# Two chains of a chunked recurrence, one head parity after the other or both side by side, on one core

## The chip, the cores and the metric

The kernel runs on one core of a Trainium2 chip. The metric is device time in microseconds: the median of three runs, and one execution more is taken with the hardware profiler. The core has a matmul engine (TensorE, PE in the rows), two elementwise engines (VectorE, DVE; ScalarE, ACT), GpSimd (POOL) and the queue that starts transfers (SyncE, SP). Each works through its own list in order and waits on semaphores. Matmul results go to eight PSUM banks of 128 x 512 floats; the other tiles lie in SBUF.

## What is computed

Two transformer blocks over 256 tokens of width 1024. The change is in the second one's time mixing, a recurrence with 8 heads of 64 dimensions; all the rest (convolution, attention, expert layers, gates) is untouched.

```python
def rwkv7_scan(r, w, k, v, a, b):
    def step(state, inp):
        rt, wt, kt, vt, at, bt = inp
        sa = jnp.einsum("bhij,bhj->bhi", state, at)
        state = state * wt[:, :, None, :] + sa[..., None] * bt[:, :, None, :] + vt[..., None] * kt[:, :, None, :]
        return state, jnp.einsum("bhij,bhj->bhi", state, rt)
    state0 = jnp.zeros((B, H, N, N), jnp.float32)
    _, ys = lax.scan(step, state0, xs)
    return jnp.swapaxes(ys, 0, 1)
...
    y = rwkv7_scan(r_h, heads(decay), k_h, v_h, -kk, kk * a_h)
    m = jnp.mean(y, axis=-1, keepdims=True)
    var = jnp.mean(jnp.square(y - m), axis=-1, keepdims=True)
    yn = ((y - m) * lax.rsqrt(var + GN_EPS)).reshape(B, S, D_RWKV)
    ...
    out = (yn + bonus) * g
...
    mixed = (gate_a * (y_attn @ w_branch_attn) + gate_b * (y_rwkv @ w_branch_rwkv)) @ w_out
```

## The kernel before

All matrices live transposed: features on partitions, tokens along a row. The recurrence isn't stepped token by token. It is done in four chunks of 64 tokens, and two chunks (128 tokens, index `a` = 0 or 1) share one set of matrices. Tiles `at_`, `bt_`, `kt_`, `rt_` hold decayed a, b, k and r: four tiles of 128 partitions, two heads in each, the even head on partitions 0 to 63 and the odd one on 64 to 127 (`q` = 0 or 1).

For each `a` and then each `q` the kernel runs one chain over four heads at a time:

- outer products over 64 partitions (`outer`, L536): `A`, `At`, `Mak`, later `Arb` and `Ark`, each masked by VectorE (L768). `At` masked to 16 x 16 blocks (L775) is the matrix to be inverted, plus identity (L779) the first `X`;
- three levels: squares `S2` and `S2t` of the block matrix (L544), copied to SBUF by ScalarE (L670, L673), and `XS`, the square times X, added to X by VectorE (L786);
- `ZV` (L552), the k part of the chunk times the values, copied by L666;
- two joining rounds, 16 to 32 and 32 to 64: `TR` transposes X (L569, copy L677), `Q` is the off-diagonal mask of `At` (L791) times that (copy L679), `XQ` is Q times X, added at L786.

After both chains of an `a` come the two chunks' state steps: `P` = a times state (L583), plus ZV (L799); `ys` = state times r (L586); `U` = X times that (L590, copy L686); `S` = k,v and b,U products (L597, L598), then VectorE adds it to the state `Sbd`, masks it to the two heads' diagonal blocks (L805) and decays it (L807). `Sbd` is 128 x 512, half of it zeros. At the end `yu` (L607, L608) gives the part of the output from U and v, copied and added into `yT` (L689, L812). Group norm statistics (L612) of y follow, then the gate columns `gb`, the branch `wb` and `w_out`.

One set of tiles (`XA`, `mS`, `mSt`, `mAt`, `mT`, `ArbT`, `ArkT`, `ZV`) serves all chains. TensorE jobs take banks 0 to 3 in turn (`take`, group A), `ys` banks 6 and 7, `yu` 4 and 5; a taken bank waits for the instruction that last read it. The order on every engine is the order of the code.

Weights come through a ring of six 1 MB slots (`ring_raw`), loaded in order by SP as soon as the unit six before has been split by ScalarE and VectorE. When the recurrence begins, `gb` 0 and 1 have been split, and their two slots hold `w_out` 0 and 1.

## Time and profile before

| | us |
|---|---|
| runs, three | 2598.78, 2600.93, 2603.32 |
| median | 2600.93 |
| profiled execution, own time | 2601.82 |
| its span, first to last instruction | 2600.1 |
| mean granted TensorE clock | 0.931 |
| recurrence, first ktok transpose to first group-norm matmul | 169.05 |

The page lists each engine's busy time; a timeline row is a start, a duration, engine, line, operation, what is written and read, and in brackets the engine's idle time before it and what ended that. An fp32 matmul leaves two records, so a job of four matmuls reads x8. The granted clock is given as a share of full speed, 1.00 or 0.50 at any moment, and a mean over a stretch.

### The profile page before, as it was taken

The page shows a single profiled execution, that of the slowest core. Times are in us where ns is not written, and L with a number is a line of the kernel's source. Part 1 is how long each engine was busy: PE and PEld are TensorE (multiplying, and loading weights), DVE is VectorE, ACT ScalarE, POOL GpSimd, SP SyncE. Part 2 cuts the span into 40 slices and gives each one's busy share as a digit, 9 for nine tenths or more (in the row PEclk, how much of TensorE's full clock was granted, in tenths as well). Part 3 has the DMA queues.
Part 4 walks back from the last instruction along what each step waited for, and adds up shares of the span by engine and source line. Part 5 has one row for each costly group of instructions (what it writes and reads, how often), then busy time and mean ns, then how long its engine had stood idle before and what let it go on. Part 6 is the DMA issues. An engine that isn't in the chain of part 4 may idle for free.

```text
span 2600.1 us, 33806 instructions
## 1 busy us (share of the span) xinstructions
PE 2342.4 (90%) x13490; PEld 1998.6 (77%) x13490; DVE 1746.8 (67%) x1709; ACT 1378.2 (53%) x1273; POOL 92.4 (4%) x147
## 2 busy tenths in 40 slices
PE   4997999799799999999999999879857786999986
PEld 3866999787688888888888888769657675888876
DVE  2764344634788888888888888554552265799954
ACT  2224333444477777777777777434421133677743
POOL 8300000001000000000000000000000000000000
PEclk6998999899799999999999999989777787999988
DMA  8566765366289999999999999766100031699940
GB/s 265 191 198 200 243 205 181 112 209 213 77 307 389 371 366 376 364 378 369 372 372 369 373 368 373 212 111 197 65 1 1 1 114 49 233 368 372 370 165 17
DMA packets 339243, 618.62 MB, mean 238 GB/s; under 512 B 24608, under 2 KB 165153, under 8 KB 339086
## 3 DMA queue, kind: packets, MB, share of 16 engines
q1 hardware_dynamic: 339086, 616.43, 67.9%
q8 instruction: 110, 1.80, 0.3%
q14 instruction: 47, 0.39, 0.0%
HBM read 614.26 MB, written 1.05 MB: 237 GB/s over the span
## 4 chain that ended last, share of the span: by engine, by line
PE 87%; DVE 7%; ACT 2%; issue 2%; SPq 1%; DMA 1%; DVEq 0%; POOL 0%; ACTq 0%; POOLq 0%
PE bank L945 10%; PE bank L946 10%; PE bank L947 10%; PE bank L1826 6%; PE bank L1827 6%; PE bank L1828 6%; PE bank L977 5%; PE bank L979 5%; PE bank L975 5%; PE bank L544 2%; PE bank L1863 1%; PE bank L1936 1%; PE bank L1897 1%; PE bank L918 1%; PE bank L1892 1%
## 5 line engine op out<-in xcount | busy, mean ns | idle before, releaser
L1150 DVE TENSOR_TENSOR ring_lo<-ring_raw,ring_hi 128x2048 fp32r<-128x2048 f32 x432 | 988.3, 2292 | 139.9 <-ACT ring_hi L1060 139.3
L1060 ACT ACTIVATE ring_hi<-ring_raw 128x2048 fp32r<-128x2048 f32 x432 | 828.1, 1920 | 288.8 <-PE bank L947 181.1
L945 PE MATMUL bank<-ring_hi,xg_hi 128*128 128x512 f32 x1152 | 458.0, 398 | 2.1 <-DVE xg_lo L1250 2.1
L946 PE MATMUL bank<-ring_hi,xg_lo 128*128 128x512 f32 x1152 | 451.0, 391 | 0.0
L947 PE MATMUL bank<-ring_lo,xg_hi 128*128 128x512 f32 x1152 | 450.8, 391 | 0.0
L1826 PE MATMUL bank<-Hh,ring_hi 128*128 128x256 f32 x1048 | 307.8, 294 | 55.9 <-DVE ring_lo L439 22.7
L439 DVE TENSOR_TENSOR ring_lo<-ring_raw,ring_hi 128x2048 fp32r<-128x2048 f32 (+1 forms) x96 | 218.0, 2282 | 189.2 <-ACT ring_hi L421 165.9
L1827 PE MATMUL bank<-Hl,ring_hi 128*128 128x256 f32 x1048 | 304.6, 291 | 0.0
L1828 PE MATMUL bank<-Hh,ring_lo 128*128 128x256 f32 x1048 | 304.1, 290 | 0.0
L1826 PEld LDWEIGHTS bank<-Hh,ring_hi 128*128 128x128 f32 x1048 | 209.6, 200 | 59.3 <-issue 48.1
L945 PEld LDWEIGHTS bank<-ring_hi,xg_hi 128*128 128x128 f32 x1152 | 217.5, 189 | 47.9 <-ACT xg_hi L1103 2.9
L947 PEld LDWEIGHTS bank<-ring_lo,xg_hi 128*128 128x128 f32 x1152 | 217.1, 188 | 47.1
L946 PEld LDWEIGHTS bank<-ring_hi,xg_lo 128*128 128x128 f32 x1152 | 217.5, 189 | 43.4
L421 ACT ACTIVATE ring_hi<-ring_raw 128x2048 fp32r<-128x2048 f32 (+1 forms) x96 | 181.4, 1898 | 109.5 <-PE bank L1828 78.8
L975 PE MATMUL bank<-ring_hi,mh 128*128 128x512 f32 x576 | 228.4, 396 | 0.0
L977 PE MATMUL bank<-ring_hi,mh 128*128 128x512 f32 x576 | 228.2, 396 | 0.0
L979 PE MATMUL bank<-ring_lo,mh 128*128 128x512 f32 x576 | 228.1, 396 | 0.0
L1827 PEld LDWEIGHTS bank<-Hl,ring_hi 128*128 128x128 f32 x1048 | 209.9, 200 | 0.1
L1828 PEld LDWEIGHTS bank<-Hh,ring_lo 128*128 128x128 f32 x1048 | 209.5, 200 | 0.0
L979 PEld LDWEIGHTS bank<-ring_lo,mh 128*128 128x128 f32 x576 | 108.4, 188 | 26.2
L977 PEld LDWEIGHTS bank<-ring_hi,mh 128*128 128x128 f32 x576 | 108.5, 188 | 25.8
L975 PEld LDWEIGHTS bank<-ring_hi,mh 128*128 128x128 f32 x576 | 108.4, 188 | 25.7
(439 smaller groups left out, 2916.6 us busy)
## 6 DMA issues: line engine op xcount, KB each, us to landing
ring_raw<-in_moe_w SPq DMA_DIRECT2D x672, 512.0 KB, 5.2
ring_raw<-in_ada_w SPq DMA_DIRECT2D x96, 512.0 KB, 5.9
ring_raw<-in_ffn_w SPq DMA_DIRECT2D x66, 512.0 KB, 5.3
ring_raw<-in_exp_gate SPq DMA_DIRECT2D x64, 512.0 KB, 5.2
ring_raw<-in_exp_up SPq DMA_DIRECT2D x64, 512.0 KB, 5.3
ring_raw<-in_exp_down SPq DMA_DIRECT2D x64, 512.0 KB, 5.6
ring_raw<-in_w_in SPq DMA_DIRECT2D x42, 512.0 KB, 4.9
ring_raw<-in_conv_in_w SPq DMA_DIRECT2D x16, 512.0 KB, 8.2
```

What stands on the lines that cost most here:

```text
L439: nc.vector.tensor_tensor(ring_lo[:, i % SPLIT, 0:kt * c], ring_raw[:, n % RAW, 0:kt * c], ring_hi[:, i % SPLIT, 0:kt * c].bitcast(F32), A ...
L945: mm(o, xg_hi[:, g, kk, :], wh(k), start=(kk == 0), stop=False)
L946: mm(o, xg_lo[:, g, kk, :], wh(k), start=False, stop=False)
L947: last = mm(o, xg_hi[:, g, kk, :], wl(k), start=False, stop=(kk == KT - 1))
L975: mm(o, mh_hi[:, 2 * h + k, :], wh[:, k, ns], start=begin, stop=False, skip_group_check=True)
L977: mm(o, mh_lo[:, 2 * h + k, :], wh[:, k, ns], start=False, stop=False, skip_group_check=True)
L979: last = mm(o, mh_hi[:, 2 * h + k, :], wl[:, k, ns], start=False, stop=end, skip_group_check=True)
L1060: run(ring_hi[:, s, :], ring_raw[:, n % RAW, :], ACT.Copy).then_inc(T.sem("hi_done"), 1)
L1150: tt(ring_lo[:, s, :], ring_raw[:, n % RAW, :], ring_hi[:, s, :].bitcast(F32), ALU.subtract).then_inc(T.sem("lo_done"), 1)
L1826: mm(o, wh[:, k, cs], Xh[:, k, :], start=(k == 0), stop=False)
L1827: mm(o, wh[:, k, cs], Xl[:, k, :], start=False, stop=False)
L1828: last = mm(o, wl[:, k, cs], Xh[:, k, :], start=False, stop=(k == kt - 1))
```

## The change

Each tile of a chain now exists twice, for q = 0 and 1: `mS`, `mAt`, `mSt` get a second copy in the bias table `relb` (rows name it relb), `mT` in `turn2`. For `a` = 1 there are `XA2`, `ZV2`, `ArbT2`, `ArkT2`, laid into the two ring slots that hold w_out 0 and 1; SP therefore loads w_out 0 only after the last `yu`. Jobs of even heads take banks 0 to 2 (`q0`), odd heads 3 to 5 (`q1`), outputs bank 6, U and S bank 7. The steps of the two chains are written side by side on all engines; the two state chunks of `a` = 0 are placed between the steps of `a` = 1; outer products are issued alternately for even and odd heads. The state `Sc` is compact, 128 x 256 without the zero blocks, so the masking pass is gone, and P, S and ys become 64 x 64 matmuls per head. y is gathered in one bank in three parts, `y_v`, `y_s`, `y_u`, and copied once by ScalarE.

```diff
+        GROUPS = {"A": [0, 1, 2, 3], "B": [4, 5], "C": [6, 7], "D": [4, 5, 6, 7],
+                  "q0": [0, 1, 2], "q1": [3, 4, 5], "state": [7], "y": [6]}
...
+            def outer(a, name, l, rr):
+                cs = slice(a * P, (a + 1) * P)
+                b = [take(pe, f"{name} {a} {q}", f"q{q}") for q in range(2)]
+                for i in range(4):
+                    for q in range(2):
+                        r = slice(64 * q, 64 * q + 64)
+                        last = mm(b[q][:, i * P:(i + 1) * P], l[r, i, cs], rr[r, i, cs], start=True, stop=True)
+                        if i == 3:
+                            last.then_inc(pe.tick(f"mm {name} {a} {q}"), 1)
...
+            def state_p(c):
...
+                for h in range(HEADS2):
+                    r, i, _ = of_head(h)
+                    last = mm(b[h % 2][b0, 64 * i:64 * i + 64], at_[r, i, t64], Sc[r, i, :], start=True, stop=True)
...
+                def body(b, h):
+                    r, i, hs = of_head(h)
+                    o = b[r, 64 * i:64 * i + 64]
+                    mm(o, ktok[b0, hs], Vtok[b0, a, hs], start=True, stop=False, skip_group_check=True)
+                    return mm(o, btok[b0, hs], U[b0, hs], start=False, stop=True, skip_group_check=True)
...
+            def y_s(c):
...
+                for h in range(HEADS2):
+                    r, i, _ = of_head(h)
+                    o = ps_y[a][r, i * P + 64 * (c % 2):i * P + 64 * (c % 2) + 64]
+                    mm(o, Sc[r, i, :], rt_[r, i, t64], start=False, stop=False,
+                       skip_group_check=True).then_inc(pe.tick(f"mm ys {c}"), 1)
...
+            tok(0)
+            strict(0)
+            squares(0, 0)
+            zv(0, 0)
+            squares(0, 1)
+            zv(0, 1)
+            reads(0)
+            for lev in range(3):
+                level(0, 0, lev)
+                level(0, 1, lev)
+            for o in range(2):
+                for step in (turn_x, joined, joined_x):
+                    step(0, 0, o)
+                    step(0, 1, o)
+
+            strict(1)
+            state_u(0)
+            squares(1, 0)
+            zv(1, 0)
+            state_s(0)
+            squares(1, 1)
+            zv(1, 1)
+            reads(1)
+            state_p(1)
+            level(1, 0, 0)
+            state_u(1)
+            level(1, 1, 0)
+            level(1, 0, 1)
+            state_s(1)
+            level(1, 1, 1)
+            level(1, 0, 2)
+            level(1, 1, 2)
+            y_v(0)
+            y_s(1)
...
+            joined_x(1, 1, 1)
+            state_u(2)
+            state_s(2)
+            state_p(3)
+            y_s(3)
+            state_u(3)
+            y_u(1)
...
+            def state_s(c):
+                dve.eng.wait_ge(*T.at(f"mm S {c}"))
+                if c:
+                    dve.eng.wait_ge(*T.at(f"mm ys {c}"))
+                tt(Sc, Sc, four(ps(f"S {c}")[:, 0:256]), ALU.add).then_inc(dve.tick(f"ev S {c}"), 1)
+                dve.eng.wait_ge(*dve.own())
+                tt(Sc, Sc, eLC[:, :, c].unsqueeze(2).to_broadcast([P, 4, 64]),
+                            ALU.mult).then_inc(dve.tick(f"S {c + 1}"), 1)
...
+                if key == ("w_out", 0):
+                    sp.eng.wait_ge(*T.at("mm yu 1"))
```

TensorE's list, at the end of the first half's second chain and the start of the state steps, before (bank numbers are PSUM banks; tB holds X, scr the state and U, GhF also Pm and the k and b columns; stat is mT, pr and prT are mS and mSt):

```order
L569 MATMUL bank0<-ident,tB 128x128 x4
L544 MATMUL bank1<-stat_54,prT 128x128 x4
L544 MATMUL bank2<-tB,pr 128x128 x4
L583 MATMUL bank3<-scr,tD 64x128 x4
L586 MATMUL bank7<-tA,scr 128x64 x4
L590 MATMUL bank0<-GhF_49,tB 64x64 x8
```

The same round after, with the first outer products of the second half behind them:

```order
L597 MATMUL bank0<-ident,tB 128x128 x4
L597 MATMUL bank3<-ident,tB 128x128 x4
L542 MATMUL bank1<-stat_54,prT 128x128 x4
L542 MATMUL bank4<-turn2_55,relb_57 128x128 x4
L542 MATMUL bank2<-tB,pr 128x128 x4
L542 MATMUL bank5<-tB,relb_57 128x128 x4
L556 MATMUL bank0<-tD,tC 128x128
L556 MATMUL bank3<-tD,tC 128x128
```

Every job has the other parity's job behind it, and the state steps have left this place; the outer products alternate between bank 0 and bank 3. Their new place on TensorE, within the second half's levels, after (L635 is U, L647 and L648 are S, L542 are S2, S2t and XS):

```order
L542 MATMUL bank0<-prT 128x128 x4
L542 MATMUL bank1<-prT 128x128 x4
L542 MATMUL bank2<-XA2_58,prT 128x128 x4
L635 MATMUL bank7<-GhF_49,tB 64x64 x8
L542 MATMUL bank3<-relb_57 128x128 x4
L542 MATMUL bank4<-relb_57 128x128 x4
L542 MATMUL bank5<-XA2_58,relb_57 128x128 x4
L542 MATMUL bank0<-pr,prT 128x128 x4
L542 MATMUL bank1<-XA2_58,pr 128x128 x4
L647 MATMUL bank7<-tB,GhF_49 64x64
L648 MATMUL bank7<-scr,GhF_49 64x64
```

U of chunk 1 now stands between the even and the odd heads' first level, and S two jobs later. VectorE's list at the start of a chain, before (L768 masks A, At, Mak, Arb, Ark; L786 adds to X):

```order
L768 TENSOR_TENSOR pr<-bank3,alibi 128x512
L768 TENSOR_TENSOR pr<-bank0,alibi 128x512
L768 TENSOR_TENSOR prT<-bank1,alibi 128x512
L775 TENSOR_TENSOR prT<-pr,alibi 128x512
L779 TENSOR_TENSOR tB<-prT,ident 128x4x128
```

and after, at the start of the second half:

```order
L929 TENSOR_TENSOR pr<-bank0,alibi 128x512
L936 TENSOR_TENSOR prT<-pr,alibi 128x512
L929 TENSOR_TENSOR relb_57<-bank3,alibi 128x512
L936 TENSOR_TENSOR relb_57<-relb_57,alibi 128x512
L929 TENSOR_TENSOR pr<-bank1,alibi 128x512
L940 TENSOR_TENSOR XA2_58<-prT,ident 128x4x128
L929 TENSOR_TENSOR relb_57<-bank4,alibi 128x512
L940 TENSOR_TENSOR XA2_58<-relb_57,ident 128x4x128
L929 TENSOR_TENSOR prT<-bank2,alibi 128x512
L929 TENSOR_TENSOR relb_57<-bank5,alibi 128x512
L971 TENSOR_TENSOR scr<-scr,bank7 128x256
L973 TENSOR_TENSOR scr<-scr,eLC 128x256
```

Six passes stand up to the first X where five stood, and the state's add and decay (L971, L973) follow before the masks of Arb.

## Rows read from the trace of the kernel before

**Rows 1.** The page, busy time, share of the span and instructions of each engine.

```profile
PE 2342.4 (90%) x13490; PEld 1998.6 (77%) x13490; DVE 1746.8 (67%) x1709; ACT 1378.2 (53%) x1273; POOL 92.4 (4%) x147
```

**Rows 2.** Table by stage of the recurrence: stretch, length, busy by engine, clock, DMA.

```profile
core 0: us, PE busy (x) PEld busy (x) DVE busy (x) ACT busy (x) POOL busy (x), PEclk, DMA share, GB/s
1906.50:1967.75 61.25, 44.46 (x312) 39.85 (x313) 20.41 (x31) 11.95 (x22) 0.00 (x0) 0.92 0.00 1
1967.75:1989.73 21.98, 18.38 (x129) 16.62 (x129) 5.53 (x8) 1.78 (x3) 0.00 (x0) 0.64 0.00 1
1989.73:2056.27 66.54, 49.77 (x315) 45.08 (x313) 19.47 (x29) 11.95 (x22) 0.00 (x0) 0.84 0.00 1
2056.27:2075.55 19.28, 14.74 (x113) 13.17 (x113) 4.14 (x6) 1.78 (x3) 0.00 (x0) 0.66 0.00 0
1906.50:2075.55 169.05, 127.36 (x865) 114.73 (x865) 49.54 (x74) 27.46 (x50) 0.00 (x0) 0.82 0.00 1
```

**Rows 3.** TensorE timeline, first half: transposes, products, a joining round, state steps.

```profile
1906.50 0.66 PE L529 MATMUL bank<-ident,tA 128*128 128x128 f32 x4 [0.87 <-DVE tD L748]
1906.99 0.60 PE L529 MATMUL bank<-ident,tC 128*128 128x128 f32 x4
...
1912.57 2.08 PE L544 MATMUL bank<-pr,prT 128*128 128x128 f32 x8 [2.10 <-DVE tB L779]
...
1949.45 2.05 PE L544 MATMUL bank<-prT 128*128 128x128 f32 x16
1951.34 1.06 PE L544 MATMUL bank<-tB,prT 128*128 128x128 f32 x8
...
1962.61 0.66 PE L569 MATMUL bank<-ident,tB 128*128 128x128 f32 x4 [0.78 <-DVE tB L786]
...
1967.75 1.09 PE L583 MATMUL bank<-scr,tD 128*64 128x128 f32 x8 [0.78 <-DVE tB L786]
...
1969.80 1.14 PE L590 MATMUL bank<-GhF,tB 64*64 64x64 f32 x16
1971.62 0.48 PE L597 MATMUL bank<-tB,GhF 64*128 64x128 f32 x2 [0.68 <-ACT scr L686]
...
1973.29 0.38 PE L598 MATMUL bank<-scr,GhF 64*128 64x128 f32 x2
1975.91 1.97 PE L583 MATMUL bank<-scr,tD 128*64 128x128 f32 x8 [2.23 <-DVE scr L807]
```

**Rows 4.** Groups by line: busy us, mean ns of one, idle before.

```profile
L679 ACT ACTIVATE pr<-bank 128x512 f32<-128x512 f32 x8 | 4.8, 597 | 10.1 <-PE bank L544 10.1
...
L2594 DVE SCALAR_TENSOR_TENSOR tA<-xT,bank 128x256 f32<-128x256 f32 x8 | 3.0, 419 | 17.1 <-PE bank L1828 17.1
```

**Rows 5.** VectorE timeline at the start of the first chain.

```profile
1910.50 0.69 DVE L768 TENSOR_TENSOR prT<-bank,alibi 128x512 f32<-128x512 f32 x1 [0.20 <-PE bank L536]
1911.11 0.68 DVE L775 TENSOR_TENSOR prT<-pr,alibi 128x512 f32<-128x512 f32 x1
1911.82 0.69 DVE L779 TENSOR_TENSOR tB<-prT,ident 128x512 f32<-128x512 f32 x1
```

**Rows 6.** TensorE's weight loads (PEld) and matmuls before the recurrence.

```profile
1868.60 0.18 PEld L508 LDWEIGHTS bank<-tB,scr 64*128 64x128 f32 x1
1868.61 0.18 PEld L510 LDWEIGHTS bank<-tB,scr 64*128 64x128 f32 x1
...
1868.61 0.48 PE L510 MATMUL bank<-tB,scr 64*128 64x256 f32 x1
...
1869.67 0.70 PE L514 MATMUL bank<-tB,scr 128*128 128x256 f32 x2
...
1871.07 0.59 PE L515 MATMUL bank<-tB,scr 128*128 128x256 f32 x2
```

**Rows 7.** Table by stage, the stretch of the second half's L607 and L608.

```profile
2070.87:2074.60 3.73, 3.73 (x32) 3.33 (x32) 0.00 (x0) 0.57 (x1) 0.00 (x0) 0.50 0.00 0
```

**Rows 8.** After the recurrence: ScalarE's split of w_out 0; SP's next transfers.

```profile
2116.77 1.90 ACT L421 ACTIVATE ring_hi<-ring_raw 128x2048 fp32r<-128x2048 f32 x1
...
2102.57 5.28 SPq L1702 DMA_DIRECT2D ring_raw<-in_w_out  x4
```

More of the change, by code:

```diff
@@ L490, in rwkv_pe, with job @@
             pe.stage = "rwkv"
-            def job(name, body, waits=()):
-                b = take(pe, name)
+            def job(name, body, waits=(), group="A"):
+                b = take(pe, name, group)
                 for label in waits:
@@ new lines, in reads, with level @@
+            def reads(a):
+                outer(a, "Arb", bt_, rt_)
+                outer(a, "Ark", kt_, rt_)
+            def level(a, q, lev):
+                n = f"{a} {q}"
+                pe.eng.wait_ge(*T.at(f"S2 {n} {lev}"))
+                power = mS[q][(lev + 1) % 2]
+                if lev < 2:
+                    job(f"S2 {n} {lev + 1}", prod(f4(mSt[q]), f4(power)), group=f"q{q}")
+                if lev < 1:
+                    job(f"S2t {n} {lev + 1}", prod(f4(power), f4(mSt[q])), group=f"q{q}")
+                pe.eng.wait_ge(*T.at(f"TX {n} {lev}"))
+                job(f"XS {n} {lev}", prod(f4(power), lambda i: XA[a][:, 2 * i + q, :]), group=f"q{q}")
@@ new lines, in state_u @@
+            def state_u(c):
+                b0, _ = by_chunk(c)
+                a = c // 2
+                if c % 2 == 0:
+                    for q in range(2):
+                        pe.eng.wait_ge(*T.at(f"TX {a} {q} 5"))
+                        pe.eng.wait_ge(*T.at(f"ev ZV {a} {q}"))
+                if c:
+                    pe.eng.wait_ge(*T.at(f"P {c}"))
+                src = Pm if c else ZV[0]
+                job(f"U {c}", each(8, lambda b, h: mm(b[b0, 64 * h:64 * h + 64], XA[a][b0, h, b0],
+                                                      src[b0, 64 * h:64 * h + 64], start=True, stop=True)), group="state")
@@ L651, in rwkv_act, with tok @@
             act.eng.wait_ge(*T.at("decayed"))
[L652 removed]
+            def tok(a):
                 for name, dst in (("ktok", ktok), ("btok", btok)):
@@ new lines, in y_out @@
+            def y_out(a):
+                act.eng.wait_ge(*T.at(f"mm yu {a}"))
+                run(yT[:, :, a * P:(a + 1) * P], four(ps(f"ys {a}")[:, :]), ACT.Copy).then_inc(act.tick(f"ev ys {a}"), 1)
+                T.mark(f"y {a}", *act.last)
+            tok(0)
+            for a in range(TT):
+                if a:
+                    state_u(0)
+                for q in range(2):
+                    zv(a, q)
+                    square(a, q, 0)
+                square(a, 0, 1)
+                if a:
+                    state_u(1)
+                square(a, 1, 1)
+                square(a, 0, 2)
+                square(a, 1, 2)
+                for o in range(2):
+                    turn_x(a, 0, o)
+                    turn_x(a, 1, o)
+                    joined(a, 0, o)
+                    joined(a, 1, o)
+                    if a and o == 0:
+                        tok(1)
+                        y_out(0)
@@ new lines, in reads, with add, off @@
+            def reads(a):
+                for name, dst in (("Arb", ArbT[a]), ("Ark", ArkT[a])):
+                    for q in range(2):
+                        masked(a, q, name, by_head(dst, q), m_iu)
+            def add(a, q, job, mark):
+                x = by_head(XA[a], q)
+                dve.eng.wait_ge(*T.at("mm " + job))
+                tt(x, x, four(ps(job)[:, :]), ALU.add).then_inc(dve.tick("ev " + job), 1)
+                T.mark(f"TX {a} {q} {mark}", *dve.last)
+            def off(a, q, o):
+                tt(four(mSt[q]), four(mAt[q]), bc4((m_o32, m_o64)[o]), ALU.mult).then_inc(dve.tick(f"off {a} {q} {o}"), 1)
@@ new lines, in state_p @@
+            def state_p(c):
+                b0 = slice(64 * (c % 2), 64 * (c % 2) + 64)
+                for q in range(2):
+                    dve.eng.wait_ge(*T.at(f"mm P {c} {q}"))
+                    dve.eng.wait_ge(*T.at(f"ev ZV {c // 2} {q}"))
+                    part = lambda t: t.rearrange("p (i q v) -> p i q v", i=4, q=2)[b0, :, q, :]
+                    tt(part(Pm), four(ps(f"P {c} {q}")[b0, 0:256]), part(ZV[c // 2]), ALU.add)                        .then_inc(dve.tick(f"ev P {c} {q}"), 1)
+                T.mark(f"P {c}", *dve.last)
```

340 lines of the change are left out of this document (176 added, 164 removed).

## Prediction, made before the changed kernel ran

> **What bounds the kernel now.** I began with the page's first lines: TensorE is busy for 2342.4 us, 90% of the span [rows 1], so only work or idle time of TensorE's in-order queue can move the end. The change touches one stretch, the recurrence, which runs from 1906.50 to the first group-norm matmul at 2075.55. The table by stage [rows 2] gives its 169.05 us in four parts: two chains of the first 128 tokens (61.25 us), their state steps and outputs (21.98), and the same for the second 128 tokens (66.54 and 19.28). TensorE is busy for 127.36 of the 169.05 us at a mean granted clock of 0.82; VectorE for only 49.54, ScalarE for 27.46, and the DMA engines move nothing. So this is one serial chain on three engines, none of which is full. The TensorE timeline [rows 3] shows why: at the end of a chain one transpose job (0.66 us), a ScalarE copy, a product, a copy, a product and a VectorE add follow one another, 5.14 us from 1962.61 to 1967.75, and nothing else is queued. The state steps are as serial: P at 1967.75, U at 1969.80, the next P at 1975.91.
>
> **Prices, all from rows.** Two product jobs of four 128x128 matmuls run from 1949.45 to 1951.34 with a third behind them: 0.94 us each; in a full queue I take 0.93; a lone one needs some 1.1 us to its last result. Four transposes take 0.49 us of queue, read from the starts 1906.50 and 1906.99 [rows 3]. A VectorE pass over 128x512 takes 0.69 us [rows 5], a ScalarE copy 0.60 [rows 4]. VectorE passes start 0.61 us apart when the later does not need the earlier (1911.11 after 1910.50), 0.71 when it does (1911.82) [rows 5]. TensorE starts 0.06 us after that last pass ends (1912.57); for handing a bank to VectorE I take 0.13 us, to ScalarE 0.04, and back 0.09. All of that is at full clock.
>
> **The outer products** (At, A, Mak, Arb, Ark; 64 partitions deep). A job of four streams as much as a product, 0.93 us, and 20 such jobs run. The change gives even heads (partitions 0 to 63) and odd heads (64 to 127) two banks and issues them matmul by matmul. The kernel already has one place like it: L508 and L510 use the two halves of the partitions. Their first weight loads start 0.01 us apart (1868.60 and 1868.61), L510's first matmul with them, and the next job starts 1.07 us after the first of these four matmuls of 256 columns; L514 and L515, 128 deep, need 1.99 us for four (1869.67 to 1871.66) [rows 6]. So I price a pair of jobs at one, 0.93 us: 10 x 0.93 = 9.3 us in place of 18.6. The other bound is no overlap, 9.3 us more.
>
> **Small state jobs.** U (eight 64x64) took 1.14 us at full clock; I keep it, 1.05 of it queue. P (now eight 64x64 in two banks and both halves) is between 0.57 and 1.14: 0.95. S has sixteen 64x64 now, bounded by half of today's 2.05 us (1971.62 to 1973.67) and two U's, 2.3: I take 1.9, since today's eight bigger ones are nearest. The outputs split in y_v and y_u (eight each) and y_s. Today's sixteen L607/L608 matmuls take 3.73 us at a granted 0.50 [rows 7], so 0.9 for eight at full clock; y_s 0.95. VectorE's state update loses a pass (the masking L805) and works on 256 columns: 128x256 passes take 0.42 [rows 4], so 0.8 for two in place of 2.1 for three of 0.69.
>
> y_s writes even and odd heads into one bank from the two halves of the array, which no row of this trace does. The Trainium skill, page "TensorEngine Tiling (Array Packing)", Gotcha 1, says that different row tiles can't access the same PSUM bank at once. By it y_s would cost U's 1.14 us rather than 0.57, an estimate of 1.7 us in all for three; my 0.95 lies near that end.
>
> **First half, in time from 1906.50.** Transposes and three outer pairs keep TensorE until 3.8. VectorE gets the first result at 2.25; six passes must be through before the first square (At, its 16-block, the same for the odd heads, A, identity added): 0.72 + 0.61 + 0.72 + 0.72 + 0.61 + 0.69 = 4.1, so 6.35. (Now 6.07 for one chain.) From there the queue is full: 4 squares, 2 ZV, 12 level jobs, 2 outer pairs, 20 x 0.93 = 18.6: 25.0. While one chain's copies and adds run, the other's matmuls do; a copy pair of 1.1 us is hidden by a level job group of 1.9 to 2.8. The first square ran at half clock (2.08 us [rows 3]) with part of the second, about 1.5 us lost, and will again: 26.5. Then two joining rounds. A round of one chain alone is 5.14. For two: the even TR starts at 0, the odd one at 1.22, since VectorE has add, mask, add to do. The even Q starts behind the odd TR at 1.71 and ends at 2.84, is copied by 3.57, and its XQ runs from 3.63 to 4.79; 0.13 + 0.69 + 0.05 later, at 5.66, the next round's TR starts. The odd Q starts at 2.70, its XQ at 4.62, in time. So two rounds take 11.3 us for both chains: 37.8. Both chains took 61.25.
>
> **Second half.** TensorE goes straight on with three outer pairs and U of chunk 0: 41.6. VectorE is free at 38.9 and needs 4.1: first square at 43.0, so 1.4 us idle. From there until the last XQ the queue sets the time, since a state step is placed two or more jobs behind the copy or add that it needs (U of chunk 1 three jobs behind P, the state update of chunk 0 done at 48.9 and used by P at 52.5): 26 product jobs 24.2, reads 1.9, transposes 2.9, two S 3.8, two P 1.9, U 1.1, five output jobs 4.5, sum 40.3: 83.3. The tail is serial: add 0.88, U 1.14, copy 0.73, S 1.9, update 0.99, P 0.95, y_s beside the Pm add 0.99, U 1.14, copy 0.73, y_u 0.95, copy 0.70, sum 11.1: 94.4. Hidden at no cost: VectorE has some 75 passes, about 47 us in 94; ScalarE 32 us.
>
> **The clock.** It is granted at one of two levels, 1.2 or 2.4 GHz. In this stretch jobs run at the lower one right after idle gaps of 2.10 and 2.23 us (1912.57: 2.08 us for one product job; 1975.91: 1.97 for P, 1.09 before) [rows 3]; the state parts ran at means of 0.64 and 0.66 [rows 2]. The new order has one gap of 2.5 us, at the start (already in), one of 1.4 and the tail with seven of 0.7 to 1.0. Lower end: no further loss. Upper end: the present mean 0.82 for the 83 us of work in the sum, 83/0.82 + 11 = 112 us. I take the 7 us of tail work mostly at half clock, +5, and 2 for the junction: 101.5, or a mean of 0.91. The gain is 169.05 - 101.5 = 67.5 us.
>
> **What is moved past a queue.** SP now waits for the last y_u before it loads w_out 0, and the 2 units (4 transfers) queue up, with the expert weights behind them. Both slots were filled before the recurrence. A transfer lands in some 5 us; ScalarE reads w_out 0 at 2116.77, 42 us after the last L608 ended, and SP was itself held until 2102.57 for w_out 2 [rows 8]. So it costs nothing; without that cover it would be two units of 5 us or less, some 8 us. What follows the recurrence is a chain from y and moves with it; the last copy of y replaces a copy plus add and is the same 0.7 us.
>
> **Sum.** The profiled execution took 2601.82 us, 0.9 above the median of 2600.93. 2601.8 - 67.5 = 2534; by the median 2533.4. I say 2534.
>
> **Rivals.** (1) The clock stays as it is now, mean 0.82: 112 us, gain 57, 2544. For it: the state steps kept TensorE busy for 18.38 of 21.98 us and still had 0.64 [rows 2]. Against: the chains, 80% of the new work, ran at 0.92 and 0.84 even with their gaps. (2) The change does not do what it says: alternating pairs do not overlap at 128 columns, since a weight load comes with every 0.11 us of streaming. +9.3 us, 2543; with (1), 2553. Against it: rows 6 show a load with every record too, at twice the columns. (3) Slower: the half clock is granted for the whole stretch. With 83 us of work at full clock the stretch takes 83/c + 11, which reaches 169 at c = 0.53; at 0.50 it is 177 us, so 8 more, 2609. For it: the state parts came near it (0.64, 0.66) with TensorE mostly busy. Against: the chains after them, from 1989.73, had 0.84 again [rows 2]. (4) All at full clock and both small-job prices at their low ends: 94.4 - 4 = 90, gain 79, 2522.
>
> **How the numbers follow.** Forecast 0.65, rival 1 0.12, rival 2 0.10 (with the first 0.03 of it), rival 4 0.09, rival 3 0.03, something between no gain and 0.2% 0.01. The range runs from 2521 to 2553: it holds the forecast, rivals 1, 2 and 4 and leaves out rival 3 and the nothing case. Faster by over 0.2% (5 us, about what a measurement of this kernel tells from no change) 0.96, within it 0.01, slower 0.03.
>
> **What would show it.** Right: about 38 us from the first ktok transpose to the second half's first outer product; L556 records of even and odd heads starting in pairs, eight in 0.9 to 1.0 us; TensorE busy over 85% between 43 and 83; VectorE waits for XS and XQ shrunk; w_out landed long before its split. Wrong: PEclk under 0.8 there, pairs in 1.8 us, or TensorE waiting on VectorE masks or ScalarE copies between the levels. If the chains turn out bound by copies, the first half is over 45 us and the forecast fails by that.

## The result, and the profile after

| | before | after |
|---|---|---|
| median of four runs, us | 2601.82 | 2531.26 |
| lowest and highest, us | 2598.78, 2603.32 | 2530.72, 2531.53 |
| profiled execution, own time, us | 2601.82 | 2531.53 |
| its span, us | 2600.1 | 2529.8 |
| mean granted TensorE clock | 0.931 | 0.938 |
| recurrence, first ktok transpose to first group-norm matmul, us | 169.05 | 95.83 |

The ratio of the medians is 0.9731, with a 95% interval of 0.9716 to 0.9745. The kernel is 70.6 us faster; the forecast was a gain of 67.5, 2534 us. The first line of the page, to set beside [rows 1]:

```profile
PE 2300.8 (91%) x13570; PEld 1964.8 (78%) x13570; DVE 1739.4 (69%) x1706; ACT 1378.0 (54%) x1273; POOL 87.0 (3%) x147
```

The table by stage of the changed kernel, to set beside [rows 2]. Its columns are the same: the stretch, its length, each engine's busy time, the granted clock. The stretches are now the first half, the second half to the end of its last XQ, and the serial tail.

```profile
1908.76:1946.48 37.72, 33.93 (x312) 32.63 (x312) 17.39 (x28) 12.17 (x22) 0.00 (x0) 0.95 0.01 1
1946.48:1991.77 45.29, 42.94 (x521) 40.05 (x520) 21.08 (x36) 13.58 (x25) 0.00 (x0) 1.00 0.01 2
1991.77:2004.59 12.82, 8.59 (x114) 7.60 (x113) 2.31 (x5) 1.78 (x3) 0.00 (x0) 0.63 0.01 1
1908.76:2004.59 95.83, 85.46 (x945) 80.28 (x945) 40.78 (x69) 27.53 (x50) 0.00 (x0) 0.93 0.01 1
```

TensorE's idle time in the recurrence fell from 41.7 us (169.05 less 127.36, [rows 2]) to 10.4 (95.83 less 85.46), its busy time from 127.36 to 85.46. ScalarE does what it did (27.53 us, 27.46 before); VectorE does 8.8 us less, 40.78 for 49.54, since the masking passes are gone and the state is half as wide. Outside of the recurrence little moved. It starts 2.26 us later in the span (1908.76 after 1906.50), and from its end to the end of the span there are 525.2 us where there were 524.6. So -73.2 + 2.3 + 0.6 = -70.3, the difference of the two profiled executions. Of the 2.3 us at the start, 1.3 are a longer wait ahead of the first ktok (2.16 us for 0.87). The other 1.0 was there before that wait, in code that the change leaves alone: the job ahead of it starts at 1901.92 before and at 1902.89 after, and in the traces of the experiments, with the same code up to there, it starts anywhere between 1899.42 and 1902.91.

TensorE's timeline of the changed kernel, to set beside [rows 3]. L547 is ktok and btok, L556 the outer products, L542 a product, L597 TR, L621 P, L635 U, L647 the first matmuls of S, L670 y_s, L741 the group norm. A pair of outer jobs leaves 16 records, and so does a job of eight small matmuls.

```profile
1908.76 0.63 PE L547 MATMUL bank<-ident,tA 128*128 128x128 f32 x4 [2.16 <-DVE tC L919]
...
1909.75 2.04 PE L556 MATMUL bank<-tD,tC 64*128 64x128 f32 x16
1911.58 1.86 PE L556 MATMUL bank<-tC,tD 64*128 64x128 f32 x16
...
1916.04 1.16 PE L542 MATMUL bank<-pr,prT 128*128 128x128 f32 x8 [1.71 <-DVE tB L940]
...
1922.74 1.16 PE L556 MATMUL bank<-tA,tC 64*128 64x128 f32 x16 [1.05 <-ACT relb L800]
...
1935.72 0.60 PE L597 MATMUL bank<-ident,tB 128*128 128x128 f32 x4
1936.80 0.66 PE L597 MATMUL bank<-ident,tB 128*128 128x128 f32 x4 [0.48 <-DVE tB L952]
...
1941.00 0.65 PE L597 MATMUL bank<-ident,tB 128*128 128x128 f32 x4
...
1946.48 1.16 PE L556 MATMUL bank<-tD,tC 64*128 64x128 f32 x16
1947.48 1.06 PE L556 MATMUL bank<-tC,tD 64*128 64x128 f32 x16
1948.37 1.06 PE L556 MATMUL bank<-tD,tA 64*128 64x128 f32 x16
1949.36 1.14 PE L635 MATMUL bank<-GhF,tB 64*64 64x64 f32 x16
1951.80 1.16 PE L542 MATMUL bank<-pr,prT 128*128 128x128 f32 x8 [1.30 <-DVE XA L940]
...
1954.70 0.34 PE L647 MATMUL bank<-tB,GhF 64*64 64x64 f32 x4
...
1955.82 2.05 PE L542 MATMUL bank<-relb 128*128 128x128 f32 x16
...
1961.75 0.68 PE L621 MATMUL bank<-scr,tD 64*64 64x64 f32 x16
1962.36 2.05 PE L542 MATMUL bank<-prT 128*128 128x128 f32 x16
...
1977.06 0.68 PE L670 MATMUL bank<-tA,scr 64*64 64x64 f32 x16
1977.67 1.09 PE L597 MATMUL bank<-ident,XA 128*128 128x128 f32 x8
...
1992.70 1.11 PE L635 MATMUL bank<-GhF,XA 64*64 64x64 f32 x16 [0.93 <-DVE XA L952]
...
1999.10 1.97 PE L635 MATMUL bank<-GhF,XA 64*64 64x64 f32 x16
...
2004.59 3.75 PE L741 MATMUL bank<-scr,uT 128*128 128x256 f32 x8 [0.78 <-ACT scr L827]
```

Read it so. Three pairs of outer jobs start at 1946.48, 1947.48 and 1948.37 and the next job at 1949.36: 2.88 us for six jobs that cost 0.93 each one by one. A joining round goes from one even TR to the next, 1935.72 to 1941.00, 5.28 us for both chains; it was 5.14 for one. Between 1951.80 and 1991.77 there is one idle gap, the 1.05 us before Arb (at 1959.77, like the one at 1922.74).

What the 73.2 us are made of can be read from the two traces, with the granted clock laid over TensorE's records. 31.3 are idle time. The other 41.9 are busy time, and there the clock has a large part: of TensorE's busy time in the recurrence, 49.9 us lay at a granted 0.50 before and 10.3 lie there now. If such work takes half as long at full clock, that is 19.8 us, an estimate; ten outer jobs less are 9.3; some 13 are left for smaller state jobs and for jobs that no longer run to their end alone.

### The profile page after: what moved, and what is told of

Its sections match the earlier page's. It is cut to its first block, busy times and chain, and to the rows that moved or that the text cites. A ratio compares the mean times of both kernels' runs of the same rounds, so it can differ in the third digit from the quotient of the medians.

```text
span 2529.8 us, 33970 instructions
## 1 busy us (share of the span) xinstructions
PE 2300.8 (91%) x13570; PEld 1964.8 (78%) x13570; DVE 1739.4 (69%) x1706; ACT 1378.0 (54%) x1273; POOL 87.0 (3%) x147
## 3 DMA queue, kind: packets, MB, share of 16 engines
HBM read 614.26 MB, written 1.05 MB: 243 GB/s over the span
## 4 chain that ended last, share of the span: by engine, by line
PE 87%; DVE 7%; ACT 2%; issue 2%; SPq 1%; DMA 1%; DVEq 0%; POOL 0%; ACTq 0%; POOLq 0%
PE bank L1131 10%; PE bank L1133 10%; PE bank L1132 10%; PE bank L2014 6%; PE bank L2015 6%; PE bank L2016 6%; PE bank L1163 5%; PE bank L1165 5%; PE bank L1161 5%; PE bank L542 2%; PE bank L2085 2%; PE bank L2051 2%; PE bank L2124 2%; PE bank L1104 1%; PE bank L2080 1%
```

## The experiments

"Recurrence" is in every case the time from the first ktok transpose to the first group-norm matmul in the trace. The kernel before, run beside them on the same chips, had medians of 2601.54 to 2602.85 us. A median is over four runs, in e12 over five, in e5 and e10 over ten.

| kernel | median us | ratio to before, 95% interval | recurrence us |
|---|---|---|---|
| the change | 2531.26 | 0.9731 (0.9716, 0.9745) | 95.83 |
| e1_outer_4_and_4 | 2533.84 | 0.9740 (0.9724, 0.9757) | 97.54 |
| e2_outer_by_parity | 2537.25 | 0.9753 (0.9737, 0.9769) | 102.88 |
| e3_state_apart | 2539.38 | 0.9762 (0.9745, 0.9778) | 104.09 |
| e4_chains_apart | 2550.93 | 0.9805 (0.9788, 0.9821) | 117.14 |
| e5_before_w_out_held | 2602.17 | 0.9999 (0.9990, 1.0009) | 169.07 |
| e6_other_first_banks | 2527.13 | 0.9712 (0.9696, 0.9729) | 94.13 |
| e7_levels_before_reads | 2530.91 | 0.9728 (0.9712, 0.9744) | 95.15 |
| e8_banks_reads_masks | 2523.33 | 0.9698 (0.9682, 0.9714) | 90.82 |
| e9_gb2_split_early | 2517.51 | 0.9674 (0.9658, 0.9690) | 90.81 |
| e10_new_jobs_old_order | 2598.60 | 0.9987 (0.9977, 0.9996) | 165.08 |
| e11_idle_work_in_tail | 2526.62 | 0.9710 (0.9694, 0.9726) | 93.38 |
| e12_all_edits | 2514.04 | 0.9659 (0.9646, 0.9672) | 88.13 |

### Each part of the change undone alone

**The alternation, matmul by matmul.** The two heads' banks and the pairing of the jobs stay; only the loops are swapped, so four even matmuls stand ahead of four odd ones.

```diff
-                for i in range(4):
-                    for q in range(2):
+                for q in range(2):
+                    for i in range(4):
```

> The changed kernel with one edit: an outer product issues the four matmuls of the even heads and then the four of the odd heads, still into two banks. Theory A (the array overlaps neighbouring jobs by itself when they use different halves of the partitions, as the L508 and L510 records show, which were issued two and two): a pair of jobs stays at 1.0 us, the recurrence at 95.8 us, the kernel at 2531 within 1.5. Theory B (issuing them in turn is what makes them overlap): ten pairs go from 1.0 to 1.9 us, the recurrence to about 105, the kernel to about 2540.

Measured 2533.84 us. TensorE's timeline of this kernel, at the second half's outer products:

```profile
1945.90 1.38 PE L556 MATMUL bank<-tD,tC 64*128 64x128 f32 x13
1947.01 0.37 PE L556 MATMUL bank<-tC,tD 64*128 64x128 f32 x1
1947.11 0.27 PE L556 MATMUL bank<-tD,tC 64*128 64x128 f32 x1
1947.22 0.27 PE L556 MATMUL bank<-tC,tD 64*128 64x128 f32 x1
1947.22 0.27 PE L556 MATMUL bank<-tD,tC 64*128 64x128 f32 x1
...
1949.75 1.14 PE L635 MATMUL bank<-GhF,tB 64*64 64x64 f32 x16
```

The three pairs take 3.85 us (1945.90 to 1949.75): more than the 2.88 with alternation, less than the 5.6 of six jobs one by one. The rows show where the rest comes from. The third job, even heads again (tC,tD), starts at 1947.01, 1.11 us after the first, where two jobs one by one take 1.86; and then records of this job and of the second one, odd heads (tD,tC), start together, both at 1947.22. So matmuls of the two partition halves overlap with no help where one group of four ends and the next, on the other half, begins; alternation makes them overlap all along. The forecast's price of one job for a pair belongs to the alternation, but its absence costs 0.3 us a pair rather than a whole 0.93. For all ten pairs the recurrence is 1.7 us longer and the kernel 2.6, so neither expectation, 2531 or 2540, came true.

**The pairing of the outer jobs.** Here At, A and Mak of the even heads stand ahead of those of the odd heads, Arb and Ark as well.

```diff
-                outer(a, "At", bt_, at_)
-                outer(a, "A", at_, bt_)
-                outer(a, "Mak", kt_, at_)
+                for q in range(2):
+                    outer(a, "At", bt_, at_, q)
+                    outer(a, "A", at_, bt_, q)
+                    outer(a, "Mak", kt_, at_, q)
```

> The changed kernel, but all outer products of the even heads are issued before those of the odd heads (At, A, Mak even, then odd; Arb, Ark even, then odd), so only one job of each group has a neighbour of the other parity. If the overlap of the two halves of the array is worth what the prediction says, six jobs take some 4.7 us in place of 3.0 and four take 2.8 in place of 2.0, and VectorE's first odd mask comes some 2 us later: 3 to 4 us per half, 6 to 8 in all, the kernel at 2538. If the pairs are hidden behind VectorE's masks anyway (TensorE waits for six passes after them), only the reads count: 2 us, 2533.

Measured 2537.25 us, 6.0 more than the change, and a recurrence of 102.88, 7.05 more. The table by stage of this kernel:

```profile
1907.57:2010.45 102.88, 97.62 (x944) 92.52 (x945) 41.15 (x69) 27.52 (x50) 0.00 (x0) 0.89 0.01 1
```

TensorE is busy 12.2 us longer (97.62 less 85.46) and idle 5.1 us less (5.26 where it was 10.37): the longer jobs fill gaps, and the mean clock is 0.89. The 9.3 us that pairing takes off the queue are worth six to seven.

**The weaving of the state steps.** The chunks 0 and 1 of the state stand between the two halves, chunk 2's P behind the last XQ.

```diff
-            strict(1)
             state_u(0)
+            state_s(0)
+            state_p(1)
+            state_u(1)
+            state_s(1)
+            y_v(0)
+            y_s(1)
+            y_u(0)
+            strict(1)
...
```

> The changed kernel without the weaving: the chains stay side by side, but U, S, P, U, S and the outputs of the first half run in one piece between the halves, and P, S, outputs of chunk 2 after the last XQ. Theory A (weaving fills the waits of the state steps): the copies and adds between them come back as idle time of TensorE, 0.7 + 1.0 + 1.0 + 0.7 and the add before U, about 5 us in the middle and 1 at the end, and some 3 to 4 us more through a lower granted clock: 2540. Theory B (the queue is full either way and the order of jobs doesn't matter): within 2 us of 2531.

Measured 2539.38 us, recurrence 104.09 (+8.3). The table by stage, the stretch of the state piece:

```profile
1943.00:1962.00 19.00, 14.28 (x209) 12.73 (x208) 5.24 (x11) 1.78 (x3) 0.00 (x0) 0.73 0.01 2
```

The piece has gaps of 0.94, 0.77, 0.97, 0.85 and 0.77 us ahead of its jobs, and ahead of the first square behind it stands one of 2.37, where the change has 1.30. Over the recurrence TensorE is idle 5.9 us more (16.2 for 10.4) and busy 2.4 us more; the expectation had 6 and 3 to 4. Weaving is worth what was expected.

**The chains side by side.** All levels and joins of the even heads run ahead of those of the odd heads.

```diff
-            for lev in range(3):
-                level(0, 0, lev)
-                level(0, 1, lev)
+            for q in range(2):
+                for lev in range(3):
+                    level(0, q, lev)
...
```

> The changed kernel with squares and outer products as they are, but levels and joining rounds of the even heads first, then those of the odd heads, in both halves; the state steps stay woven in. Theory A (most of the gain is one chain's copies and adds lying under the other's matmuls): each half's levels and rounds go from about 22 us to 2 x 17 in the first half, +10 to 13; in the second the woven jobs fill part, +6 to 10; together +18 to 22, the kernel at about 2551. Theory B (the gain is mostly overlap in the array, smaller state jobs and a higher clock): +5 or less.

Measured 2550.93 us, recurrence 117.14 (+21.3); over it TensorE is busy for 91.88 us at a mean clock of 0.93, as in the change. TensorE's timeline of this kernel, a joining round of one chain:

```profile
1931.62 0.66 PE L597 MATMUL bank<-ident,tB 128*128 128x128 f32 x4 [0.78 <-DVE tB L952]
1933.01 1.13 PE L542 MATMUL bank<-stat,prT 128*128 128x128 f32 x8 [0.73 <-issue]
1934.82 1.16 PE L542 MATMUL bank<-tB,pr 128*128 128x128 f32 x8 [0.69 <-ACT pr L814]
```

These are the gaps of the kernel before, back one for one. Its TensorE timeline has, behind the transposes at 1962.61 [rows 3],

```profile
1964.00 1.13 PE L544 MATMUL bank<-stat,prT 128*128 128x128 f32 x8 [0.73 <-issue]
1965.81 1.16 PE L544 MATMUL bank<-tB,pr 128*128 128x128 f32 x8 [0.69 <-ACT pr L679]
```

This is the largest single part of the gain. Of the 21.3 us, 14.9 are idle time (117.14 less 91.88 is 25.3, where the change has 10.4); the other 6.4 are busy time. Most of that is that a job with nothing queued behind it takes 1.13 us to its end and not 0.9 to the next start. The clock has a small part: 14.6 us of the busy time lie at a granted 0.50, where the change has 10.3, so some 2 us, an estimate.

**All the order at once.** The new jobs (compact state, small matmuls, y in three parts, the new tiles) stay, and the order of the kernel before returns: chain after chain, outer jobs by parity, state steps at the end of each half.

```diff
-            tok(0)
-            strict(0)
-            squares(0, 0)
-            zv(0, 0)
-            squares(0, 1)
...
+            for a in range(TT):
+                tok(a)
+                for q in range(2):
...
```

> The jobs of the changed kernel (compact state of 256 columns, P, S and outputs per head, its banks and second set of tiles) in the order of the kernel before: one chain after the other, outer products by chain, state steps after each half. It tells order from content. If content is only the smaller state jobs, as the prediction prices them (a state part of 22 and one of 19 us become about 12 and 13), the recurrence takes 169 - 16 = 153 us and the kernel 2585, so the order is worth 54 us. If the parts measured so far (side by side 21, weaving 8, paired outer products 7) just add up, the order is worth 37 and this kernel comes to 2568.

Measured 2598.60 us, 3.0 below the kernel before that ran beside it (2601.61), with an interval that just leaves out no change: both numbers expected were too low. The table by stage, cut as [rows 2]:

```profile
1906.69:1976.36 69.67, 53.07 (x312) 48.71 (x313) 18.22 (x28) 12.17 (x22) 0.00 (x0) 0.78 0.00 1
1976.36:1989.54 13.18, 10.27 (x161) 9.11 (x161) 3.15 (x7) 1.18 (x2) 0.00 (x0) 0.75 0.00 1
1989.54:2056.73 67.19, 50.59 (x314) 46.10 (x312) 18.09 (x27) 12.87 (x23) 0.00 (x0) 0.82 0.00 1
2056.73:2071.77 15.04, 11.17 (x162) 9.88 (x161) 3.05 (x7) 1.78 (x3) 0.00 (x0) 0.65 0.01 2
1906.69:2071.77 165.08, 125.10 (x945) 113.81 (x945) 42.50 (x69) 28.00 (x50) 0.00 (x0) 0.78 0.00 1
```

The new state jobs save 8.8 us in the first state part (21.98 to 13.18) and 4.2 in the second (19.28 to 15.04), 13 in all. The chains give 9 back: 61.25 became 69.67 and 66.54 became 67.19. Two things in the trace account for that: waits of 0.96 us ahead of Arb for a ScalarE copy, four of them (3.8 us), since three banks rotate where four did; and low clock, 0.78 instead of 0.92 in the first chains, where now the outer jobs and first squares run at 1.2 GHz (the first outer job takes 2.02 us, behind the same wait of 2.15 at the start that the change has; before it took 1.16 behind 0.87).

Against the change this kernel's recurrence is 69.25 us longer, with the same 945 records: 29.6 of that is idle time (39.98 against 10.37) and 39.6 is busy time (125.10 against 85.46). Ten outer jobs that no longer lie beside another are 9.3 of the busy time; the other 30 us are the same matmuls taking longer. Most of that is the clock: at a granted 0.50 lie 63.1 us of this kernel's busy time and 10.3 of the change's, and half of the difference is 26 us, an estimate. The 4 us that are left fit the ends of lone jobs, as in e4. The three single undoings above add 7.05, 8.3 and 21.3, together 36.6. So the order's parts are worth more together than apart: with one of them undone the clock stays at 0.89 or above, with all undone it falls to 0.78. Of the surplus, 1.7 us are e10's own, four waits ahead of Arb (3.8 us) where the change has two (2.1).

### Rivals that a single run could settle

**The transfer that is moved.** In the kernel before, SP alone is changed: it loads w_out 0 only behind the last yu.

```diff
+                if key == ("w_out", 0):
+                    sp.eng.wait_ge(*T.at("mm yu 1"))
```

> The kernel before with one edit: SP waits for the last yu before it loads w_out 0, as in the changed kernel; its ring slots aren't used for anything else. If the load is hidden, as predicted (w_out 0 is read 42 us later), the time is the same, 2601 within 2. If it delays the split of w_out or the expert weights behind it, +5 us or more.

Measured 2602.17 us, ratio 0.9999 (0.9990 to 1.0009). The hold costs nothing. In the changed kernel SP issues the held transfers at 2003.84, and the ScalarE split that stood at 2116.77 [rows 8] stands at 2045.78.

**The bank at the start.** TensorE waits 2.16 us before the first ktok, and did 0.87 [rows 3]. The row names a VectorE pass, L919, which reads the last bank of a job before the recurrence; the VectorE timeline of the changed kernel has it as

```profile
1907.33 1.28 DVE L919 TENSOR_TENSOR tC<-tB,bank 128x512 f32<-128x512 f32 x2
```

and ktok, the first job of group q0, takes that bank. The edit lets both groups begin one bank further.

```diff
-                  "q0": [0, 1, 2], "q1": [3, 4, 5], "state": [7], "y": [6]}
+                  "q0": [1, 2, 0], "q1": [4, 5, 3], "state": [7], "y": [6]}
```

> The changed kernel with the rotation of the two bank groups shifted by one (1, 2, 0 and 4, 5, 3), so that the first ktok transposes no longer take the bank that the bonus products (rk) are read from. Theory A (the 2.16 us of idle time before the first transpose, 0.87 in the kernel before, is the wait for that bank): the recurrence starts 1.3 to 2.2 us earlier, the kernel comes to 2529. Theory B (VectorE is late there anyway and its first mask waits for its own queue): VectorE is free at 1908.9 in either order, so the chain gains under 0.5 us.

Measured 2527.13 us, 4.1 less than the change. TensorE's timeline of this kernel:

```profile
1906.53 0.66 PE L547 MATMUL bank<-ident,tA 128*128 128x128 f32 x4 [0.85 <-DVE tD L912]
...
1907.55 1.16 PE L556 MATMUL bank<-tD,tC 64*128 64x128 f32 x16
1908.54 1.06 PE L556 MATMUL bank<-tC,tD 64*128 64x128 f32 x16
```

The wait is 1.3 us shorter, as expected, and the recurrence behind it is 1.7 us shorter too (94.13): 0.85 up to the first square and 0.85 in the tail. The outer pairs now run at 2.4 GHz from the first one (1.16 and 1.06 us), where after a wait of 2.16 they ran at 1.2 GHz (2.04 and 1.86). That is 3.0 of the 4.1 us. The rest isn't shown to be the edit's: in this trace the job ahead of the wait starts 0.94 us earlier than in the change's (1901.95, 1902.89), in code that is the same and whose start differs by as much from trace to trace.

**The two gaps before Arb.** Arb of the odd heads takes the bank of the odd square S2, and ScalarE may copy that square only when Mak, in the same tile, has been read by ZV. So ScalarE's order is ZV, then square, as its timeline of the changed kernel shows, and TensorE waits for the copy that starts at 1922.01:

```profile
1921.73 0.38 ACT L794 ACTIVATE GhF<-bank 128x256 f32<-128x256 f32 x1 [1.32 <-PE bank L575]
1922.01 0.59 ACT L800 ACTIVATE relb<-bank 128x512 f32<-128x512 f32 x1
```

The edit puts the first even level job between.

```diff
+            level(0, 0, 0)
             reads(0)
-            for lev in range(3):
+            level(0, 1, 0)
+            for lev in range(1, 3):
...
```

> The changed kernel with the first level of the even heads issued before Arb and Ark (and U of chunk 1 one job later), in both halves. The trace shows TensorE idle for 1.05 us twice before Arb, waiting for ScalarE to empty the bank of the odd heads' square. If that is the cause, both gaps go: -2 us, 2529. If the wait moves to the next job, which needs another bank or the same copy, no change.

Measured 2530.91 us, no different from the change. Both gaps are gone, but see the table by stage, and TensorE's first square of the second half in its timeline:

```profile
1907.16:1943.79 36.63, 33.92 (x312) 32.62 (x312) 17.39 (x28) 12.05 (x22) 0.00 (x0) 0.95 0.01 1
1943.79:1989.80 46.01, 44.72 (x521) 41.65 (x520) 21.05 (x36) 13.46 (x25) 0.00 (x0) 0.96 0.01 2
```

```profile
1949.12 2.01 PE L542 MATMUL bank<-pr,prT 128*128 128x128 f32 x8 [1.29 <-DVE XA L942]
```

The first half is 1.1 us shorter, the second 0.7 longer with 1.8 us more busy time and a mean of 0.96 for 1.00: that square ran at 1.2 GHz behind a gap of 1.29 us, where in the change it ran at 2.4 GHz behind one of 1.30. The gap was the same; what TensorE had done ahead of it wasn't. I can't say from these rows what tips it.

### What is left to gain

**Both edits, and masks by parity.** e8 has the edits of e6 and e7, and VectorE makes all masks of the even heads before those of the odd heads, so that the even square can start after four passes.

```diff
-                dve.eng.wait_ge(*dve.own())
-                for q in range(2):
+                    made = dve.own()
                     masked(a, q, "A", four(mS[q][0]), m_sl16)
+                    dve.eng.wait_ge(*made)
...
```

> The changed kernel with three edits: the bank rotation and the level before the reads as in the two kernels before this one, and VectorE's masks per parity (At, block, A, X, Mak even, then odd), so that the first square waits for four passes, not six. If the parts add up: 1.5 to 2.2 for the start, 2.1 for the two gaps, 1.1 per half for the masks, together 5 to 6.5 us, the kernel at 2525.5. If the masks only move the wait to the odd heads' square, 3 to 4 us, 2528.

Measured 2523.33 us, recurrence 90.82: 2.2 us below the lower of the two numbers expected. The wait ahead of the first square is 1.01 us, where it was 1.71 in the change and 2.47 in e6.

**The unit behind the group norm.** In the changed kernel TensorE stands idle for 5.42 us, in the gate columns, for the split of gb 2 on VectorE:

```profile
2031.45 0.55 PE L2014 MATMUL bank<-Hh,ring_hi 128*128 128x256 f32 x1 [5.42 <-DVE ring_lo L452]
```

ScalarE and VectorE have that split behind the group norm in their lists, though the weights have long been there. e9 is e8 with the split placed in the first half of the recurrence, where both engines have slack.

```diff
+            split_hi(act, at_unit[("gb", 2)])
...
+                if not a:
+                    split_lo(dve, at_unit[("gb", 2)])
```

> The kernel with the three edits (banks, level before reads, masks by parity) and one more: the weight unit gb 2 is split in hi and lo during the first half of the recurrence, where ScalarE and VectorE wait for 5 us and more, not after the group norm. In the changed kernel TensorE is idle for 5.4 us between 2022 and 2032, waiting for that split. Theory A (that split alone is late): the idle time goes, 5 us less, 2518. Theory B (gb columns aren't on the path; the branch wb waits for the group norm's result and for its own split anyway, so TensorE only waits later): under 1.5 us, 2522.

Measured 2517.51 us, 5.8 less than e8. The wait for gb 2, 5.87 us in e8, is gone, and one of 2.01 stands 48 matmuls later, ahead of the next unit. That makes 3.9 us; the rest isn't divided. TensorE's timeline of this kernel:

```profile
2025.72 0.35 PE L2019 MATMUL bank<-Hh,ring_hi 128*128 128x256 f32 x1 [2.01 <-DVE ring_lo L452]
```

**Matmuls that compute nothing.** e11 is the change with identity matmuls, whose result nobody reads, in the five waits of the tail (three in each) and ten between the two group-norm jobs.

```diff
+            def idle_work(n):
+                b = bank[T.banks["Q 1 0 1"]]
+                for _ in range(n):
+                    mm(b[:, 0:P], ident[:, :], ident[:, :], start=True, stop=True)
...
+            idle_work(3)
             state_u(2)
...
```

> The changed kernel with matmuls of the identity by itself, into a bank that nobody reads, while TensorE waits in the tail: three (0.7 us) before U, S, P, y_u and the first group-norm job of the last chunks, and ten after the first group-norm jobs. The tail runs at a granted 0.63 now, the group norm's first jobs at 3.75 us in place of some 1.9. Theory A (the clock falls because TensorE idles there): the tail from the last XQ to the group norm goes from 12.8 to 9.5 us, the group-norm jobs save 2 to 2.5, the kernel comes to 2526. Theory B (the low clock comes from small 64x64 jobs, or the added work delays the real jobs as much as it helps): within 1.5 us of 2531, or slower.

Measured 2526.62 us, 4.6 less than the change. TensorE's timeline of this kernel:

```profile
1989.91 0.83 PE L685 MATMUL bank<-ident 128*128 128x128 f32 x6
1991.01 1.11 PE L635 MATMUL bank<-GhF,XA 64*64 64x64 f32 x16 [0.26 <-DVE XA L965]
...
1996.62 1.14 PE L635 MATMUL bank<-GhF,XA 64*64 64x64 f32 x16 [0.39 <-DVE GhF L977]
...
2000.44 1.97 PE L751 MATMUL bank<-scr,uT 128*128 128x256 f32 x8
```

U of chunk 3 takes 1.14 us where it took 1.97, the first group-norm job 1.97 where it took 3.75: the whole tail is at 2.4 GHz. From the end of the last XQ, 1990.08, to the group norm it takes 10.4 us, where the change takes 12.8 and the expectation had 9.5. So theory A holds, with a smaller gain in the tail than it said. Part of the gain is lost again, since the wait for gb 2 grows by a microsecond to 6.43.

**All of it.** e12 is e9 with the matmuls of e11.

> The kernel with the bank rotation, the level before the reads, masks by parity and gb 2 split early (2517.5), plus the added identity matmuls in the tail, which alone took the changed kernel from 2531.3 to 2526.6. If they act on a part that the other four edits leave as it was: 4 to 5 us less, 2513. If TensorE, now without its wait for the split of gb 2, waits for the group norm instead, the tail's gain is partly lost there: 2515 to 2517.

Measured 2514.04 us, ratio 0.9659 (0.9646 to 0.9672): 17.2 us below the change and the fastest of all. The identity matmuls gain 3.5 us here and 4.6 alone; the wait for the unit behind gb 2 is 2.57 us with them and 2.01 without. The recurrence takes 88.13 us, all of it at a granted 1.00.

## Why the prediction was right, point by point

**The bound.** It held that the stretch was one serial chain on three engines and that only TensorE's idle time and queue counted. e4 shows it: with the chains apart, the gaps of 0.69 to 0.83 us return, and 21 us.

**The first half, 37.8 us.** Measured 37.72 (1908.76 to 1946.48), but its steps are off, by +0.9, -1.5, +1.1 and -0.5 us, and cancel; that the sum fits is luck. The clock fell earlier than forecast, in the outer pairs (2.04 and 1.86 us) and not in the first square (1.16), so the square started at 7.3 instead of 6.35 and the 1.5 us for its half clock didn't come. The queue behind it, priced at 20 jobs of 0.93 = 18.6, took 19.7 from 1916.04 to 1935.72; without the gap of 1.05 before Arb it is 18.6. Two joining rounds took 10.8 us, not 11.3, since the odd TR starts 1.1 us after the even one rather than 1.22. The gap was the missed step: I took three banks for a group as enough and didn't follow the bank of S2 to the copy that empties it.

**The second half, 45.5 us to the last XQ, and 2 for the clock at the junction.** Measured 45.29 with nothing for the clock (1.00). Priced too high: S at 1.9 us, measured 1.1 (1954.70 to 1955.82); P at 0.95, measured 0.61 (1961.75 to 1962.36); y_s at 0.95, measured 0.61 (1977.06 to 1977.67). For two S, two P and two y_s that is 3.0 us. S has sixteen small matmuls and costs what U's eight do: its even and odd heads read the same partitions but write different ones, and their records start in pairs 0.01 us apart (1954.70 and 1954.71), as those of P and y_s do. Missed: the second gap of 1.05; the other 1.7 us are y_v and y_u at 1.03 for 0.9 and products that start 0.99 apart where something had to be waited for, not 0.93. U (1.07, 1965.24 to 1966.31) and the outer pairs (0.9 to 1.0) came as priced.

**The tail, 11.1 us at full clock and 5 for the clock.** Measured 12.82 at a mean of 0.63. e11 divides the two: its tail at full clock, 1990.08 to 2000.44, takes 10.4 us, so the jobs were priced 0.7 too high (S and P again), and the clock took 2.5, not 5. U of chunk 2 (1.11 us) and half of S still ran at 2.4 GHz.

**The start, not in the sum.** The recurrence began 1.3 us late for a bank, and the half clock behind it cost 0.85 us up to the first square. e6 took both away, and in its trace 0.85 us of the tail with them: 3.0 us, of 4.1 in the medians. This term was missed altogether, though the order of banks stood in the code and the engine that reads rk last could be read off.

**The mean clock,** 0.91 assumed, was 0.93. Rival 1 (0.82 all through) and rival 3 (0.5) are refuted for this order. But e10 has 0.78 with the same jobs in the old order, so the clock did depend on the order, as the sum assumed without an experiment to lean on. Rival 4 was half right: the small jobs came in near its low prices, the full clock did not come. In e12, at full clock and with four edits more, the recurrence takes 88.13 us; rival 4 said 90.

**Rival 2, no overlap of pairs,** is refuted: records of even and odd heads start 0.01 us apart in pairs (1946.48 and 1946.49). Without alternation 1.0 us of the 2.7 that no overlap would cost for three pairs comes (e1). **The transfer** was hidden, as stated (e5).

**y_s in one bank.** Its even and odd heads write one bank from the two halves of the array. It takes 0.61 us, and its first two records start at 1977.06 and 1977.07; P, whose halves write two banks, takes 0.61 as well. My price was 0.3 us too high each time. The Trainium skill, page "TensorEngine Tiling (Array Packing)", Gotcha 1, says that different row tiles can't access the same PSUM bank at once; by it y_s would have cost about U's 1.07, an estimate. This trace doesn't agree.

In sum: 5.7 us less in the recurrence than forecast, 2.3 later at its start, 0.6 more behind it, so 2.8 us less than 2534.3: 2531.5. The mechanism held, and each part of it is measured; that the total came within 3 us is in part luck, since jobs priced 3.7 us and a clock priced 4.5 us too high (2 at the junction, 2.5 in the tail) stand against the gap and the dearer jobs of the second half, the bank at the start and a later start that isn't the change's.

## What to carry to other kernels

Where one chain bounces between three engines, count the gaps of one round and put a second independent chain in them, each with its own tiles and banks: here that is the largest part of the gain, and it brings the clock along. Then follow every PSUM bank to the instruction that empties it, at the start of the stretch above all, since a wait of 1.3 us there cost about 3. Two matmuls that each use half of the partitions are worth one if they are issued alternately.

## What of the hardware was unexpected

- Without alternation, fp32 matmuls on the two partition halves still overlap across a job boundary: 3.85 us for three pairs, between 2.88 and 5.6 (e1). There the third job's first record (tC,tD, 1947.01) starts before records of the second (tD,tC, 1947.11 and 1947.22), so matmuls on different halves don't start strictly in the order of the list.
- Two matmuls of different partition halves that write one bank are no slower than with two banks: 0.61 us for eight heads of 64x64 (y_s and P), with the records of two heads starting 0.01 us apart.
- A gap removed can cost clock elsewhere: e7 closed two gaps of 1.05 us and had a square at 1.2 GHz in return, behind a gap of the same 1.3 us as in the change. e6 closed 1.3 us and won 3.0 in the trace.
- Identity matmuls in a tail of waits turned jobs of 1.97 us into 1.14 and the group norm's 3.75 into 1.97, for 4.6 us of the whole (e11). In e12, which has them too, the recurrence never leaves the full clock.
